# A two-block transformer on one core: zeros multiplied while x is loaded, halves of x taken from the banks, lambda's sums moved

## The reference

```python
# first block
h = rmsnorm(x, norm1_g)
proj = h @ w_in            # q, k, v, forget logits, pool input u
attn = forgetting_attention(q, k, v, log_sigmoid(f_logit + b_forget))
pool = multiscale_pool(u, w_pool, pool_scale)      # windows of 2, 4, 8, 16
x = x + concat(attn, pool) @ w_out
h2 = rmsnorm(x, norm2_g)
x = x + (silu(h2 @ w_gate) * (h2 @ w_up)) @ w_down
x = rmsnorm(x, final_g)
# second block, layer 0: differential attention
lam = exp(sum(lq1 * lk1)) - exp(sum(lq2 * lk2)) + 0.2
a = softmax(s1) - lam * softmax(s2)
# then a convolutional FFN; layer 1: latent attention and the same FFN; a last norm
```

## Time and profile before

| | |
|---|---|
| median of 3 runs | 1857.08 us (1857.0 to 1858.16) |
| profiled execution | 1857.17 us |
| its span, first to last instruction | 1855.4 us |
| PE busy | 1826.2 us, 98% |
| DVE busy | 1135.3 us, 61% |
| ACT busy | 792.6 us, 43% |
| mean granted clock of PE | 0.996 |

### The profile page before, as it was taken

The page is one execution under the profiler, slowest core; times in us unless marked ns, Lnnn a source line. Parts: engine busy times, 40 slices in busy tenths (PEclk is TensorE's granted clock), DMA queues, the critical chain, the costliest instruction groups (busy, mean ns, idle before and its releaser), DMA issues.

```text
span 1855.4 us, 23103 instructions
## 1 busy us (share of the span) xinstructions
PE 1826.2 (98%) x8954; PEld 1517.2 (82%) x8954; DVE 1135.3 (61%) x1886; ACT 792.6 (43%) x1407; POOL 160.7 (9%) x155
## 2 busy tenths in 40 slices
PE   8999999999999999999999999999999999999998
PEld 6897788888888898987888888879888888888886
DVE  4577644344346777768663663665889866366364
ACT  5563332222135555454441432446767544144242
POOL 4003200000004101012000000023010200000002
PEclk9999999999999999999999999999999999999999
DMA  4211223323322221112333333232111133332332
GB/s 147 79 47 55 77 92 101 92 91 95 98 91 94 69 69 57 47 57 86 92 95 91 96 98 91 92 87 69 37 46 35 61 99 95 99 91 92 100 93 80
DMA packets 127961, 152.17 MB, mean 82 GB/s; under 512 B 9258, under 2 KB 100940, under 8 KB 127852
## 3 DMA queue, kind: packets, MB, share of 16 engines
q1 hardware_dynamic: 127692, 150.62, 26.3%
q10 hardware_dynamic: 160, 0.07, 0.0%
HBM read 148.50 MB, written 2.10 MB: 81 GB/s over the span
## 4 chain that ended last, share of the span: by engine, by line
PE 92%; DVE 4%; POOL 2%; issue 1%; ACT 1%; DMA 0%; POOLq 0%; DVEq 0%; ACTq 0%
PE bk L1552 23%; PE bk L1554 23%; PE bk L1553 23%; PE bk L1580 5%; PE bk L1581 5%; PE bk L1582 5%; PE bk L1557 3%; PE bk L1635 1%; PE bk L1637 1%; PE bk L1636 1%; DVE R L1676 1%; PE bk L1614 1%; DVE XT L1697 1%; PE bk L1641 1%; PE bk L1621 1%
## 5 line engine op out<-in xcount | busy, mean ns | idle before, releaser
L1552 PE MATMUL bk<-R,WH 128*128 128x512 f32 x1812 | 720.8, 398 | 9.0 <-DVE WL L1685 4.3
L1553 PE MATMUL bk<-R,WH 128*128 128x512 f32 x1812 | 716.6, 395 | 0.0
L1554 PE MATMUL bk<-R,WL 128*128 128x512 f32 x1812 | 716.5, 395 | 0.0
L1685 DVE TENSOR_TENSOR WL<-RAW,WH 128x1024 fp32r<-128x1024 f32 (+3 forms) x282 | 352.0, 1249 | 542.6 <-ACT WH L1855 541.9
L1855 ACT ACTIVATE WH<-RAW 128x1024 fp32r<-128x1024 f32 (+3 forms) x282 | 293.5, 1042 | 702.2 <-PE bk L1554 640.5
L1552 PEld LDWEIGHTS bk<-R,WH 128*128 128x128 f32 x1812 | 340.4, 188 | 91.5 <-DVE WL L1685 4.7
L1554 PEld LDWEIGHTS bk<-R,WL 128*128 128x128 f32 x1812 | 340.2, 188 | 83.3
L1553 PEld LDWEIGHTS bk<-R,WH 128*128 128x128 f32 x1812 | 340.4, 188 | 80.9
L1980 POOL TENSOR_TENSOR FS<-FS 128x512 f32<-128x512 f32 x56 | 88.7, 1591 | 1252.2 <-ACT FS L1879 1249.9
L1580 PE MATMUL bk<-WH,R 128*128 128x512 f32 (+4 forms) x528 | 188.1, 356 | 2.5 <-DVE R L1676 2.5
L1581 PE MATMUL bk<-WH,R 128*128 128x512 f32 (+4 forms) x528 | 181.2, 343 | 0.0
(11 more groups left out here) (126 smaller groups left out, 1653.6 us busy)
## 6 DMA issues: line engine op xcount, KB each, us to landing
RAW<-in_ffn_w_up_dram SPq DMA_DIRECT2D x176, 256.0 KB, 3.0
RAW<-in_ffn_w_down_dram SPq DMA_DIRECT2D x44, 512.0 KB, 3.8
RAW<-in_w_gate_dram SPq DMA_DIRECT2D x44, 256.0 KB, 2.8
RAW<-in_w_up_dram SPq DMA_DIRECT2D x44, 256.0 KB, 3.1
RAW<-in_w_down_dram SPq DMA_DIRECT2D x22, 512.0 KB, 3.6
RAW<-in_da_w_qkv_dram SPq DMA_DIRECT2D x32, 256.0 KB, 3.0
RAW<-in_w_in_dram SPq DMA_DIRECT2D x17, 256.0 KB, 3.1
RAW<-in_w_out_dram SPq DMA_DIRECT2D x8, 512.0 KB, 3.6
```

The lines of the kernel that those rows point to most:

```text
L1552: e.matmul(dst, lh, rh, start=start, stop=False)
L1553: e.matmul(dst, lh, rl, start=False, stop=False)
L1554: return e.matmul(dst, ll, rh, start=False, stop=stop)
L1685: e.tensor_tensor(WL[:, s, 0:m], RAW[:, r, 0:m], WH[:, s, 0:m].bitcast(F32), ALU.subtract).then_inc(on["wlo_dve"], 1)
```

## The change

Three things are changed, and some durations of the planner's model with them.

First, a strand `warm` puts matmuls of zeros (64 rows of a zeroed KT tile, 512 columns) into PE's list wherever the model leaves PE idle before the first product of x and w_in. Landing times in the model are set anew.

Second, each tile of x is split straight from the bank it was turned in, once norm1_g's columns are there; the copy into XT and the square come after. At most three such banks are held at first (`cap["one"] = 3`), then four. The first two chunks of w_in are cut to half (one tile of 128 rows each), and both are loaded ahead of the second quarter of x. The order in which POOL zeroes KT begins with the tile that `warm` reads.

Third, `spawn(lam_sums())` stands behind the pool products of the forgetting part instead of behind the first FFN.

```diff
+        if kind == "warm":
+            return 430.0
-        return {"whi": 1060.0, "tap2": 805.0, ...
+        if kind == "whi":
+            return 210.0 + 0.83 * f["m"]
-            return dve(n) if f["scale"] is None else 1.45 * dve(n) if f["src"].shape[0] == P and n == S else 1.1 * dve(n)
+            return dve(n) if f["scale"] is None else 1.45 * dve(n) if f["from_x"] else 1.1 * dve(n)
+        if kind == "wlo":
+            return 175.0 + 1.07 * f["m"]
...
-            plan_qk(w_in, g, 0, 512)
+            plan_qk(w_in, g, 0, 512, (2, 2, 2, 2) if g else (1, 1, 2, 2, 2))
...
-            landing(s_x[q], (5000.0, 8500.0, 12000.0, 13500.0)[q])
-        coming(0, 1700.0)
-        coming(1, 5500.0)
+            landing(s_x[q], (5000.0, 7800.0, 9300.0, 10800.0)[q])
+        landing(s_n1, 4000.0)
+        coming(0, 0.0)
+        coming(1, 0.0)
+        ready_at[id(s_raw[0]), landed[0]], ready_at[id(s_raw[1]), landed[1]] = 5700.0, 6400.0
+        wires[0] = 9000.0
+        def warm():
+            st, i = None, 2
+            b = yield from bank("gemm")
+            ready_at[id(k_zeros[0][0]), k_zeros[0][1]] = 1300.0
+            while not made.get("gemm_t_pe", 0):
+                st = yield step("warm", bank=b.i, i=i, after=[k_zeros[0]])
+            kfree[i].append(st.pe)
+            put_bank(b, st.pe)
...
-            if f % 2:
-                st = yield step("x_copy_a", f=f, bank=b.i, after=[st.pe])
-                x_done[f] = [st.act]
-            else:
-                st = yield step("x_copy_v", f=f, bank=b.i, after=[st.pe])
-                x_done[f] = [st.dve]
-            put_bank(b, *x_done[f])
             while not flags.vec:
                 yield None
-            N.feed(f)
+            yield from fill(N.X[f])
+            cut = yield from split_pair(N.X[f], BK[b.i][:, :], [turned.pe], col(V_N1 + f))
+            spawn(x_copy(f, b, cut))
+        def x_copy(f, b, cut):
+            st = yield step("x_copy_a" if f % 2 else "x_copy_v", f=f, bank=b.i, after=[cut])
+            x_done[f] = [st.act if f % 2 else st.dve]
+            put_bank(b, *x_done[f])
+            cap["one"] = 4
+            N.feed(f, made=True)
...
+        spawn(vectors(0, V_N2), 0)
+        spawn(warm(), 4)
+        cap["one"] = 3
         for f in range(8):
-            spawn(x_in(f), 0)
-        spawn(vectors(0, V_N2), 0)
+            spawn(x_in(f), 0 if f < 2 else 0.6)
-        spawn(high_weights(range(1)), 0)
-        spawn(low_weights(range(1)), 0)
-        hot += [spawn(high_weights(range(1, len(chunks))), 2), spawn(low_weights(range(1, len(chunks))), 2)]
+        spawn(high_weights(range(2)), 0)
+        spawn(low_weights(range(2)), 0)
+        hot += [spawn(high_weights(range(2, len(chunks))), 2), spawn(low_weights(range(2, len(chunks))), 2)]
...
             N.free_x(newest_use())
             N.shut = True
+            spawn(lam_sums())
             yield from till(A0)
...
             spawn(settle(ND))
-            spawn(lam_sums())
...
             load(0)
+            load(1)
             e.dma_start(TOK[:, :, 256:512], xq[:, :, 256:512]).then_inc(s_x[1], 16)
-            load(1)
...
+                elif k == "warm":
+                    for done in st.after:
+                        w.wait_ge(*done)
+                    e.matmul(BK[st.bank][:, :], KT[0:64, st.i, 0:P], KT[0:64, st.i, :], start=True, stop=True).then_inc(on["warm_pe"], 1)
```

More of the change, by code:

```diff
@@ L182, in takes @@
             return 420.0 + 440 + 1.55 * width_of(f["p1"])
-        return {"wlo": 1273.0, "add": 682.0, "tap1": 743.0, "tap0": 743.0, "settle": 745.0, "diag": 880.0, "root_in": 165.0,
+        if kind == "wlo":
+            return 175.0 + 1.07 * f["m"]
+        return {"add": 682.0, "tap1": 743.0, "tap0": 743.0, "settle": 745.0, "diag": 880.0, "root_in": 165.0,
                 "root_out": 760.0, "both_in": 370.0, "both_out": 370.0, "eighth": 170.0, "lam_in": 500.0, "lam": 500.0,
@@ L374, in drop, with halves, split_pair @@
             tiles.put(pair.l, *done)
-        def halves(dst_h, dst_l, src, after, scale=None, free=()):
+        def halves(dst_h, dst_l, src, after, scale=None, free=(), from_x=False):
             hi = yield step("hi", dst=dst_h, src=src, scale=1.0 if scale is None else scale, after=counts([*after, *free]))
-            lo = yield step("lo", dst=dst_l, src=src, high=dst_h, scale=scale, after=[hi.act])
+            lo = yield step("lo", dst=dst_l, src=src, high=dst_h, scale=scale, from_x=from_x, after=[hi.act])
             return lo.dve
-        def split_pair(pair, src, after, scale=None, rows=slice(0, P)):
+        def split_pair(pair, src, after, scale=None, rows=slice(0, P), from_x=False):
             h, l = pair.h, pair.l
-            lo = yield from halves(R[rows, h.i, :], R[rows, l.i, :], src, after, scale, h.free + l.free)
+            lo = yield from halves(R[rows, h.i, :], R[rows, l.i, :], src, after, scale, h.free + l.free, from_x)
             pair.ready = [lo]
@@ L402, in build, with plan_qk @@
         up2, dn2 = a["ffn_w_up_2"], a["ffn_w_down_2"]
-        def plan_qk(w, g, qo, ko):
-            for k in range(0, 8, 2):
-                chunk(2, 512, (0, wap(w, k * P, 2, qo + g * 256, 256)), (256, wap(w, k * P, 2, ko + g * 256, 256)))
+        def plan_qk(w, g, qo, ko, nks=(2, 2, 2, 2)):
+            k = 0
+            for n in nks:
+                chunk(n, 512, (0, wap(w, k * P, n, qo + g * 256, 256)), (256, wap(w, k * P, n, ko + g * 256, 256)))
+                k += n
         def plan_v(w, g, vo, extra):
@@ L485, in high_weights @@
                 free = [w_used[n - NSP]] if n >= NSP else []
-                w_split[n] = yield step("whi", n=n, after=[(s_raw[n % NRAW], landed[n]), *free])
+                w_split[n] = yield step("whi", n=n, m=chunks[n][0] * chunks[n][1], after=[(s_raw[n % NRAW], landed[n]), *free])
         def low_weights(which):
@@ L492, in low_weights @@
                 st = w_split[n]
-                lo = w_low[n] = yield step("wlo", n=n, after=[st.act])
+                lo = w_low[n] = yield step("wlo", n=n, m=chunks[n][0] * chunks[n][1], after=[st.act])
                 if n + NRAW < len(chunks):
@@ L565, in __init__, with feed @@
                 spawn(self.total(), 0)
-            def feed(self, f):
-                if self.split:
+            def feed(self, f, made=False):
+                if self.split and not made:
                     spawn(self.make(f))
@@ L576, in make @@
                 sc = self.cols[:, f:f + 1] if self.cols is not None else col(self.g + f)
-                yield from split_pair(self.X[f], XT[:, f, :], x_done[f], sc)
+                yield from split_pair(self.X[f], XT[:, f, :], x_done[f], sc, from_x=True)
             def square(self, f, which):
@@ L700, in build @@
         k_zeros = [emit("k_zero", lo=64 if hh % 2 == 0 else 0, i=s * 8 + hh * 2 + x).pool
-                   for s in range(2) for hh in range(4) for x in range(2)]
+                   for s in range(2) for hh in (1, 0, 3, 2) for x in range(2)]
         kfree = [[k_zeros[-1]] for _ in range(16)]
@@ L712, in build @@
         flags.consts = flags.vec = flags.conv = False
+        def warm():
[6 more added lines that the diff above has]
+            put_bank(b, st.pe)
         def x_in(f):
             c = f // 4
-            while c and not flags.vec:
-                yield None
             b = yield from bank()
             src = [TOK[:, t, f * P:f * P + P] if c == 0 else FS[:, xs2[t].i, (f - 4) * P:(f - 3) * P] for t in range(4)]
-            st = yield step("x_turn", bank=b.i, src=src, after=counts([b.free, (s_x[f // 2], 16)]))
+            turned = yield step("x_turn", bank=b.i, src=src, after=counts([b.free, (s_x[f // 2], 16)]))
             if f < 4:
-                tok_free.append(st.pe)
+                tok_free.append(turned.pe)
             if f == 7:
                 for x in xs2:
-                    fsl.put(x, st.pe)
-            if f % 2:
-                st = yield step("x_copy_a", f=f, bank=b.i, after=[st.pe])
-                x_done[f] = [st.act]
-            else:
-                st = yield step("x_copy_v", f=f, bank=b.i, after=[st.pe])
-                x_done[f] = [st.dve]
-            put_bank(b, *x_done[f])
+                    fsl.put(x, turned.pe)
             while not flags.vec:
                 yield None
-            N.feed(f)
+            yield from fill(N.X[f])
[7 more added lines that the diff above has]
+            N.feed(f, made=True)
         def vectors(lo, hi):
@@ L790, in put @@
                 for (i, r), hi in zip(parts, his):
-                    st = yield step("lo", dst=KT[r, i + 1, :], src=bank[r, :], high=KT[r, i, :], scale=None, after=[hi])
+                    st = yield step("lo", dst=KT[r, i + 1, :], src=bank[r, :], high=KT[r, i, :], scale=None, from_x=False, after=[hi])
                     kready[i] = [st.dve]
```

4 lines of the change are left out of this document (2 added, 2 removed).

## The result

The changed kernel takes 1861.57 us (median of 11 runs, 1860.33 to 1864.33) against 1857.11 us before (median of 11): a ratio of 1.0023, 95% interval 1.0015 to 1.0030. It is slower by 4.5 us where 1856.4 was forecast and 1861.5 was the upper end of the range. (The ratios here are the record's own and not the quotients of the medians; the two can differ by 0.0004.) The profiled execution took 1861.42 us with a span of 1859.6 us, 4.2 us over the span before.

What follows compares the result with a forecast made beforehand. PE, 92% of the chain that ended last, was taken to bound the kernel. 1857.17 - 3.3 (start) + 4.0 (pool stage) - 1.4 (norm) = 1856.5, less 0.1 to the median: 1856.4 us; range 1851.0 to 1861.5.

Steps and rivals of the forecast that it cites:

- The start: Kernel start: zeros, halves from banks and half chunks let 24 products, not 10, be done by 20.0 us; -3.3 us.
- what they may give is the clock: Start: zeros delay turn 0 by 2.5 us but may raise PE's clock at 9.5 to 10.1 us.
- the zeros do nothing: Rival, start: clock rises no sooner than before (19.0 us), start gains 0, total 1859.7 us; chance 0.08.
- The pool stage: Before `mix`: lambda's sums delay a half by 2.5 us and a low clock costs 1.5 us; +4.0 us.
- A gap of 2.5 us left the clock up here: Pool stage: the old 2.5 us wait kept the clock, so a longer wait's low clock is new; 1.5 us.
- The first rival: Pool stage: lambda's sums cost nothing there, total 1852.4 us; chance 0.31.
- The norm: Second block's norm, near 603 us: without `lam` there, wait goes and low clock is half counted; -1.4 us.
- The 0.6 us go: Second block's norm: POOL ends about 1.2 us sooner, so PE's wait of 0.61 us vanishes.
- The changed model durations ... only move the order of the list: Planner's model: new durations for weights and the split of `mixed` only reorder the list; no term in the sum.
- The slower rival: Sums cost full price in a pool stage of about 8.4 us; total 1861.5 us; chance 0.15.
- With the bounds above this case reaches from 1853.5 to 1860.5: Whole kernel: span in us given for the main forecast case from the bounds of its terms.

Runs made afterwards that it cites:

- e4: e1 with the fourteen filling products reading 128 rows of zeros instead of 64; 1854.53 us, ratio 0.9988.
- e2: e1 with no strand `warm`, so without the zeros; 1854.86 us, ratio 0.9991.
- e5: The kernel before with only lambda's sums moved into the pool stage; 1856.88 us, ratio 0.9997.
- e8: The changed kernel with the planner's old durations everywhere but in the start; 1858.26 us, ratio 1.0004.
- e9: The changed kernel with its fourteen filling products reading 128 rows of zeros; 1857.56 us, ratio 1.0004.
- e10: e4 (old durations outside the start) with lambda's sums spawned behind `mix`; 1853.93 us, ratio 0.9980.
- e12: The kernel before with lambda's sums in the pool stage and the planner's new durations, start as before; 1860.30 us, ratio 1.0019.
- e6: The kernel before with only the planner's new durations for weight halves and for splits taking a scale from a bank; 1859.10 us, ratio 1.0008.
- e1: The changed kernel with lambda's sums back behind the first FFN and old durations outside the start; 1858.56 us, ratio 1.0010.
- e7: The changed kernel with lambda's sums moved back behind the first FFN; 1858.15 us, ratio 1.0007.

## Why the prediction was wrong

Two steps failed. The clock's rise in the start was put at 9.5 to 10.1 us and came at 14.68, which left -0.7 us of -3.3. And the planner's new durations were put at nothing, where the pair of profiles shows +2.4 us in the latent attention.

**The start, -3.3 forecast.** The failed step is "what they may give is the clock": it put the rise at 9.5 to 10.1 us by rows of products of 128 rows, and took over the pace for 64 rows without asking whether the clock answers to them. It came at 14.68. With 128 rows it comes at 7.0 to 9.6 and the start is at -3.7 to -4.6. That is near the forecast in part by luck of the draw, since the profile of before has the slowest start of five; against their mean it is -2.5 to -3.5. Nine zeros ahead of turn 0 (8.62 for a forecast 8.25) and halves from the banks held. Chunk 2 is split at 19.8 us in e4 for a forecast of 20.0, and is what PE waits for in e2, but in the changed kernel its halves are ready at 22.8 only, when PE is late itself and doesn't wait for them. As it is, the start is at -1.0 to +0.4 at 47 us in four profiles, the old one at 0.0 to -1.9 in five; their means are -0.25 and -1.15. The zeros cost what they stand in the way of. The rival "the zeros do nothing" had the mechanism, with a chance of 0.08.

**The pool stage, +4.0 forecast, +2.8 in this pair.** The place and the low clock came as forecast, 3.4 us at 0.50, and the wait grew by half of what was said: to 3.8 us for a forecast of about 5, 1.2 us more than before for 2.5. Two things in it were wrong. The price of the sums came from rows that stood beside POOL; with POOL at rest the steps take 0.22 and 0.16 us, so their time was POOL's, and it is not owed again when they stand elsewhere. And e5 shows that they cost 0.3 us here, if the order stays. The rest came through the planner's durations, which I had put aside. The low clock was booked as new because one profile had kept the clock through 2.5 us; six of nine profiles with that wait lose it, so the kernel before probably pays for it in many of its runs. "A gap of 2.5 us left the clock up here" is the step that one profile can't carry. The first rival, sums for nothing, holds for the sums alone (e5), but not for the change.

**The norm, -1.4 forecast, -0.3 in this pair.** In the table it is the step from 595 to 1286 us: +2.3 to +2.0 in the changed kernel, and -0.1 to -0.3 us in e5, e8, e9, e10 and e12, where the sums have left too. The wait shrank from 0.61 to 0.39 us, and the clock fell at 612.0 as it had at 609.5; it does so in every profile here. The step that failed is "The 0.6 us go": POOL's eight additions now run without a gap, 13.39 us from 595.53 on, and PE waits for the last of them. The upper end of the bound, 0, was nearly right.

**What was left out.** "The changed model durations ... only move the order of the list": they cost 2.2 us in e6 by the medians, through a low clock in the latent attention, some 1300 us behind the start. That term stood in the diff and had no place in the sum.

**The slower rival** gave 1861.5, and 1861.57 was measured, but not by its mechanism: it wanted 8.4 us in the pool stage. The stages show +2.8 there and +2.4 elsewhere.

**The range.** "With the bounds above this case reaches from 1853.5 to 1860.5" doesn't follow from them: all low ends together give 1850.8 us, all high ends 1862.3, and it isn't said how the range was narrowed.

What stays open: the parts add up only roughly. The start alone (e1, +1.8 us) and the rest alone (e12, +3.2 us) make 4.9 us by the medians, where the change has 4.5. e7 to e1 says that the new durations cost nothing beside the new start (1858.15 and 1858.56), e6 that they cost 2.2 us beside the old one. e7's runs lie in two groups, 1856.6 to 1859.4 and 1861.3 to 1862.3, and the mean granted clock on record goes with them: 0.995 or 0.996 in the four runs up to 1856.90, 0.993 and 0.992 in the two longest. So long runs are runs with more time at the low clock; in which stage they had it is not on record, and there the account is argued and not shown.

## What to carry to other kernels

Before filling an idle PE, ask of every filler what waits behind it in the queue, and have it use the whole array: half of it took as long and left the clock down. Then compare with no filler at all; here that was as good (e2 and e4). A step's time beside a busy POOL is POOL's, so it is no price for the step in another place; look for the same step where POOL rests. Where a list is made by a planner, a change of its model is an edit to every stage, and it needs a term of its own.

## What the runs showed of the hardware

- Products of 64 rows and 512 columns took 0.43 us each, as those of 128 rows at that clock do (3.35 us for seven of either), but the clock came up 10.7 to 13.1 us after the first, against 3.5 to 6.0 us for 128 rows. Zeros and ones made no difference: 9.47 and 9.55 us.
- The same wait keeps the clock in one profile and loses it in another: one of 2.5 us at the same product lost it in six of nine profiles, two waits of 0.68 and 0.95 us in three of six. In the five profiles of the old start the rise lay between 15.35 and 19.02 us. Such a draw is 1.0 to 1.6 us in the pool stage (from 47 to 186 us in the table), about 2.2 us in the latent attention and up to 1.9 us in the start, where part of it is the landing of x: as much as most parts of this change.
- A sum of products over 64 columns on DVE, with both inputs in SBUF, took 0.22 us with POOL at rest and 1.07 to 1.31 us beside POOL's additions. The Trainium skill, "SBUF — State Buffer", section "Who interferes with whom", says that a DVE instruction with two inputs in SBUF contends with a GpSimd instruction that reads SBUF; the runs agree for this instruction too, which the rows of the kernel before alone had left to be inferred.
